# Token halves at the end of each output projection, and earlier evictions in the filter loop

## The reference, cut to what matters

```
x = x + (silu(h @ w_ffn_gate[l]) * (h @ w_ffn_up[l])) @ w_ffn_down[l]
return rmsnorm(x, norm_final)
...
a = attention(rms_norm(h, pre)) @ w_o
h = h + rms_norm(a, a_norm_post[l])
f = conv_ffn(rms_norm(h, ffn_norm_pre[l]))
h = h + rms_norm(f, ffn_norm_post[l])
...
def conv_ffn(x, w_in, conv_w, conv_b, w_out):
    u = x @ w_in
    u = causal depthwise conv of width 3 over tokens (u) + conv_b
    gate, val = jnp.split(u, 2, axis=-1)
    return (jax.nn.gelu(gate) * val) @ w_out
```

## Time and profile before

| what | value |
|---|---|
| median of 3 runs | 2651.42 us (2649.61 to 2651.51) |
| profiled execution, its own time | 2651.55 us |
| its span in the trace | 2649.7 us |
| PE busy | 2523.8 us, 95% of the span |
| POOL busy | 1615.3 us, 61% |
| DVE busy | 1382.1 us, 52% |
| ACT busy | 748.6 us, 28% |
| mean granted clock of PE | 0.982 of full speed |

### The profile page before, as it was taken

How to read it: one execution, slowest core, us unless ns; L and a number is a source line. 1 busy time by engine, 2 the same in 40 slices (tenths; PEclk the granted TensorE clock), 3 DMA queues, 4 the chain that set the end, 5 groups by cost and what they waited for, 6 DMA issues and landing times. The chain is left out here.

```text
span 2649.7 us, 37177 instructions
## 1 busy us (share of the span) xinstructions
PE 2523.8 (95%) x12786; PEld 2077.5 (78%) x12786; DVE 1382.1 (52%) x1995; ACT 748.6 (28%) x1398; POOL 1615.3 (61%) x1548
## 2 busy tenths in 40 slices
PE   8889999999999999999999799999999999999998
PEld 6678878788877888888777577888877777778886
DVE  6656675454423533320477658774064444687722
ACT  2255444001132221100334433331032222343300
POOL 6546555664544777777544267887763333778874
PEclk9999999999999999999999899999999999999999
DMA  4333323332222333323322122333222211233321
GB/s 140 120 96 100 95 84 95 89 92 68 68 64 98 93 95 98 96 96 99 108 64 65 36 78 82 99 95 99 85 76 81 68 64 48 84 87 95 98 96 64
DMA packets 235784, 229.20 MB, mean 86 GB/s; under 512 B 15809, under 2 KB 228289, under 8 KB 235665
## 3 DMA queue, kind: packets, MB, share of 16 engines
q1 hardware_dynamic: 212224, 204.72, 25.9%
q10 hardware_dynamic: 23440, 22.82, 3.0%
HBM read 222.67 MB, written 4.82 MB: 86 GB/s over the span
## 5 line engine op out<-in xcount | busy, mean ns | idle before, releaser
L583 POOL TENSOR_SCALAR whi<-raw 128x512 fp32r<-128x512 f32 x772 | 561.3, 727 | 943.9 <-issue 514.4
L585 POOL TENSOR_TENSOR wlo<-raw,whi 128x512 fp32r<-128x512 f32 x772 | 1055.7, 1368 | 64.4
L625 PE MATMUL PS<-opA_hi,whi 128*128 128x512 f32 x1872 | 751.5, 401 | 21.5 <-DVE fu L1939 9.5
L625 PE MATMUL PS<-opA_hi,wlo 128*128 128x512 f32 x1872 | 735.9, 393 | 0.0
L625 PE MATMUL PS<-opA_lo,whi 128*128 128x512 f32 x1872 | 735.5, 393 | 0.0
L625 PEld LDWEIGHTS PS<-opA_hi,whi 128*128 128x128 f32 x1872 | 356.0, 190 | 110.7 <-issue 21.6
L625 PEld LDWEIGHTS PS<-opA_hi,wlo 128*128 128x128 f32 x1872 | 355.1, 190 | 76.5
L625 PEld LDWEIGHTS PS<-opA_lo,whi 128*128 128x128 f32 x1872 | 356.0, 190 | 71.5 <-issue 1.5
L1949 DVE SCALAR_TENSOR_TENSOR facc<-fu,vec,facc 128x512 f32<-128x512 f32 x176 | 208.5, 1243 | 24.4 <-ACT facc L1322 24.2
L619 PE MATMUL PS<-whi,opA_hi 128*128 128x256 f32 x704 | 207.0, 294 | 0.0
L619 PE MATMUL PS<-whi,opA_lo 128*128 128x256 f32 x704 | 200.2, 284 | 0.0
(11 more groups left out here) (314 smaller groups left out, 3399.8 us busy)
## 6 DMA issues: line engine op xcount, KB each, us to landing
raw<-in_w_in_dram SPq DMA_DIRECT2D x184, 256.0 KB, 2.7
raw<-in_ffn_w_in_dram SPq DMA_DIRECT2D x176, 256.0 KB, 2.8
raw<-in_ffn_w_out_dram SPq DMA_DIRECT2D x88, 256.0 KB, 2.6
raw<-in_a_w_qkv_dram SPq DMA_DIRECT2D x48, 256.0 KB, 2.7
raw<-in_w_ffn_gate_dram SPq DMA_DIRECT2D x44, 256.0 KB, 2.8
raw<-in_w_ffn_up_dram SPq DMA_DIRECT2D x44, 256.0 KB, 2.8
raw<-in_w_ffn_down_dram SPq DMA_DIRECT2D x44, 256.0 KB, 2.6
acs_row<-acs_dram ACTq DMA_DIRECT2D x16, 512.0 KB, 5.9
```

Source lines behind the costliest of these rows:

```text
L583: nc.gpsimd.tensor_scalar(whi[slot][:], raw[raw_slot][:], 1.0, 1.0, ALU.mult, ALU.mult).then_inc(w_high, 1)
L585: nc.gpsimd.tensor_tensor(wlo[slot][:], raw[raw_slot][:], whi[slot][:].bitcast(F32), ALU.subtract).then_inc(slab_split, 1)
L625: last = nc.tensor.matmul(psum_fm(key, panel, m), a, b[:, k, :], start=k + n == 0, stop=k == total - 1 and n == 2)
```

## The change

The last tile (m = 1) of each of the five projections is computed in two halves of 256 tokens, the second into a bank of `AUX`; in the projections of eleven slabs this holds for all slabs of the last panel. The norm follows by halves: the factors of the first half are formed while PE computes the second, and DVE, ACT and PE treat the first two tiles (the first four at the end, k = 10) of the next operand in halves. `keep_warm` is gone from these boundaries. In the filter loop the eviction of half 1 moves from between the two `taps` of its own pass to the end of the pass before.

```diff
+HALVES = {2: 2, 4: 2, 6: 2, 8: 2, 10: 4}
+TOKENS = slice(0, HS), slice(HS, S)
...
+        def tail(key, h):
+            return psum_fm(key, 3, 1)[:, TOKENS[0]] if h == 0 else AUX[:, 0, TOKENS[1]]
...
+            def spread_late(k):
+                pe.wait_ge(rstd_ready, k + 1)
+                pe.wait_ge(half_res, HALF0[k] + HALVES[k])
+                for t in range(2, NB):
+                    last = nc.tensor.matmul(AUX[:, 3, t * P:(t + 1) * P], rstd_col[:, t:t + 1].broadcast_to([P, P]), ident[:], start=True, stop=True)
+                last.then_inc(bc_done, 1)
...
-            def branch_norm(k):
-                sum_squares(k)
-                keep_warm(WARM_FACTORS)
-                spread(k)
-                keep_warm(WARM_RESIDUAL)
...
+            def last_panel_norm(key, k):
...
+                for kk in range(first):
+                    s = slab_no(key, panel, kk)
+                    pe.wait_ge(slab_split, s + 1)
+                    for c in range(SLAB):
+                        products(psum_fm(key, panel, 0), s, c, 0, SLAB * kk + c, slice(0, S))
+                        for h in range(2):
+                            last = products(tail(key, h), s, c, 1, SLAB * kk + c, TOKENS[h])
...
             def prepare(k, dst, name, first, src_ready):
+                for c in range(HALVES[k - 1]):
+                    act.wait_ge(half_res, HALF0[k - 1] + c + 1)
+                    A(dst[:, c, TOKENS[0]], XT[:, c, TOKENS[0]], ACT.Copy, scale=col(name, first + c)).then_inc(half_hi, 1)
+                    if c == 0:
+                        norm_late(k - 1)
+                    A(next_squares[:, TOKENS[0], c], XT[:, c, TOKENS[0]], ACT.Square).then_inc(next_sq, 1)
...
+            def chunks(scale, add, k, ready0, nxt, first, late):
...
+                factors_half(k)
+                for c in range(H):
+                    scale(c, 0)
+                    if nxt and c:
+                        low_half(c - 1)
+                    add(c, 0)
+                    if c == 0:
+                        late()
+                factors_late(k)
                 if nxt:
+                    low_half(H - 1)
+                dve.wait_ge(bc_done, k + 1)
+                for c in range(DC):
+                    tokens = TOKENS[1] if c < H else slice(0, S)
+                    scale(c, 1 if c < H else None)
+                    if nxt and c:
+                        next_low(*nxt, c - 1, ready0, TOKENS[1] if c - 1 < H else slice(0, S))
+                    add(c, 1 if c < H else None)
...
+                def late():
+                    done(key, 3)
+                    dve.wait_ge(sq_ready, SQUARES0[k] + DC + 1)
+                    V.tensor_copy(branch[:, DC - 1, TOKENS[1]], tail(key, 1)).then_inc(tail_res, 1)
...
                 products(0)
+                evict(1, 1)
                 with dve.Fori(1, FP - 1) as i:
                     taps(i, 0)
-                    evict(i, 1)
                     taps(i, 1)
                     dve.wait_ge(fconv_tap, 88 * l + 8 * i + 4)
                     evict(i, 0, 1)
                     products(i)
+                    evict(i, 1, 1)
```

More of the change, by code:

```diff
@@ L624, in chunk @@
                     for n, (a, b) in enumerate(((ah, hi), (ah, lo), (al, hi))):
-                        last = nc.tensor.matmul(psum_fm(key, panel, m), a, b[:, k, :], start=k + n == 0, stop=k == total - 1 and n == 2)
+                        last = nc.tensor.matmul(psum_fm(key, panel, m)[:, tokens], a, b[:, k, tokens], start=tokens.start == 0 and k + n == 0,
+                                                stop=k == total - 1 and n == 2, skip_group_check=skip)
                 return last
@@ L634, in twin_mm @@
                 ready, base = FIRST_USE[key]
-                order = [(t, c) for c in range(total - 2) for t in (a, b)] + [(a, total - 2), (a, total - 1), (b, total - 2), (b, total - 1)]
+                first = 0
+                if norm in NEXT:
+                    first = HALVES[norm - 1]
+                    for h in range(2):
+                        for c in range(first):
+                            for t in (a, b):
+                                s = slab_no(*t, c // SLAB)
+                                if h == 0:
+                                    if c % SLAB == 0:
+                                        pe.wait_ge(slab_split, s + 1)
+                                    if t == a:
+                                        pe.wait_ge(half_op, HALF0[norm - 1] + c + 1)
+                                elif t == a:
+                                    pe.wait_ge(ready, base + c + 1)
+                                last = chunk(*t, s, c % SLAB, c, total, TOKENS[h], True)
+                                if h == 1 and c % SLAB == SLAB - 1:
+                                    last.then_inc(slab_done, 1)
+                            if h == 0 and c == 0:
+                                spread_late(norm - 1)
+                order = [(t, c) for c in range(first, total - 2) for t in (a, b)] + [(a, total - 2), (a, total - 1), (b, total - 2), (b, total - 1)]
                 for t, c in order:
@@ L709, in sum_squares @@
                 else:
-                    pe.wait_ge(acc_ready, ADDED0[k] + (DC - 1 if k in BRANCHES else DC))
+                    pe.wait_ge(acc_ready, ADDED0[k] + DC)
                 for t in range(NB):
-                    last = nc.tensor.matmul(AUX[:, 3, t:t + 1], acc[:, t * P:(t + 1) * P], ones[:, 0:1], start=t == 0, stop=k not in BRANCHES,
-                                            skip_group_check=True)
[L714 to L718, removed]
@@ L1872, in _, with next_low @@
             add_squares(2, 6)
-            done("down1", 3)
-            down_residual(7)
-            def next_low(name, first, c, ready0):
+            dve.wait_ge(tail_done, 1)
+            V.tensor_tensor(XT[:, DC - 1, TOKENS[0]], XT[:, DC - 1, TOKENS[0]], tail("down1", 0), ALU.add).then_inc(evicted, 1)
+            def next_low(name, first, c, ready0, tokens):
                 dve.wait_ge(res_ready, ready0 + c + 1)
-                low(opA_lo[:, c, :], XT[:, c, :], col(name, first + c), opA_hi[:, c, :])
@@ L1881, in chunks @@
[L1881 to L1890, removed]
-                if nxt:
-                    next_low(*nxt, DC - 1, ready0)
+                low(opA_lo[:, c, tokens], XT[:, c, tokens], col(name, first + c), opA_hi[:, c, tokens])
@@ L1901, in residual, with down_late @@
+            def down_late():
+                done("down1", 3)
+                V.tensor_tensor(XT[:, DC - 1, TOKENS[1]], XT[:, DC - 1, TOKENS[1]], tail("down1", 1), ALU.add).then_inc(tail_res, 1)
+            chunks(lambda c, h: None, final_norm, 2, 0, ("a_norm_pre_2", 0), (("q2", 0), [q2[0][:, m, :] for m in range(2)]), down_late)
             def residual(key, k, name, first, nxt, layer, first_panel):
```

173 lines of the change are left out of this document (136 added, 37 removed).

## The result

The changed kernel takes 2658.24 us (median of 9 runs, 2656.69 to 2659.53), the kernel before 2651.37 us (9 runs on the same chip, 2649.61 to 2653.74). The ratio is 1.0028, 95% interval 1.0018 to 1.0038, so it is about 7 us slower, which is clear of noise though small. The prediction was 2647.2. The profiled execution has a span of 2656.1 us, 6.4 more than before, and a mean granted clock of 0.977 where it was 0.982.

What follows compares the result with a forecast made beforehand. PE is busy 95% of the span, but DVE sets the end of the boundary stage. Terms -9.7 + 1.5 + 1.6 + 0.7 + 1.7 = -4.2 us give 2647.3, stated as 2647.2; own range 2644 to 2650, 8 in 10: 2641 to 2654.

Steps and rivals of the forecast that it cites:

- The step that failed: `bwo` boundary: PE ends 12 half products at 11.05, spreads the second half, DVE goes on at 11.75 after 0.6 idle.
- The second rival: Boundaries without constant matmuls: PE idles, the clock falls, each of four pays 1.7, +6.8 in all, 2654; chance 12%.
- the first scale: `bwo` boundary: DVE's first scale at 7.05 after tile m = 1 begins, 2.1 earlier than 9.18.
- the first product: `bwo` boundary: PE starts the next projection at about 9.6, 2.8 earlier than before.
- PE's head start: `bwo` boundary: PE's 2.8 us are given back whole to DVE; the stage ends 0.3 to 0.7 later.
- `awo`, `fout 0` and `bwo`: Boundaries behind these three projections: +0.5 each, +1.5 together, with POOL adding to DVE's extra half steps.
- Behind `down1`: Boundary after `down1`: +1.6, ACT on the path with an Exp and two table loads of 1.28.
- A last panel of eleven slabs: Split products of the first seven slabs, 42 in each of three projections: 0.55 longer each, +1.7 together.
- The end: End of the kernel (k = 10): +0.7, with 0.8 of DVE waiting for the late spread.
- the filter loops: Two filter loops with the moved eviction: gain of 4.85 each, -9.7, two waits of 1.2 to 2.4 replacing 4.75.
- no half-speed products behind: Sign in the filter loops: PE's remaining waits for the fu evictions are not followed by products at half speed.
- the attentions: Attentions 1 and 2: no term in the forecast sum; the result's table lists their forecast as 0.

Runs made afterwards that it cites:

- The kernel with the loop alone: Kernel before with only the new order of evictions in the filter loop, boundaries as before: 2641.95 us, ratio 0.9968.
- the two with the Exp moved: Changed kernel with constants in PE's waits, late spread sooner and two Exp ahead of `down1`'s squares: 2648.3 us; with both loop evictions early too: 2640.32 us.
- The token halves with the old loop: Changed kernel with the old order of evictions in the filter loop, so only the token halves remain: 2662.28 us, ratio 1.0039 to before.
- the kernel before with the prompt loop: Kernel before with both filter loop evictions as early as their panels are there, boundaries as before: 2640.1 us, ratio 0.9953.

## Why the prediction was wrong

**The step that failed** is in the boundary: "PE ends 12 half products at 11.05, then spreads the second half, so DVE can go on at 11.75: 0.6 idle". It takes PE at full clock behind the new waits. In the runs they are followed by half speed at all four boundaries of the changed kernel (behind `awo` from the fifth product on), and PE is on DVE's path here, through the late spread. So 12 products of 0.213 take 2.7 instead of 1.4 and the spread 0.3 more; DVE goes on at 13.44 and idles 2.37. With constants in the waits this is undone (11.89) and the whole kernel is level with before.

The second rival ("the clock falls in the new gaps", 12%, 2654) had the mechanism. It priced a boundary at 1.7, from the earlier trace rows; against my own steps the four measured 1.0 to 1.7 more each, 5.3 in all. The Trainium skill, page "TensorE: Matmul & The Clock Gate", section "What's actually happening", says that activity releases the throttle and that throttled is the default. By that rule the constants do work though they compute nothing; the run without them (+9.0) agrees. I had given the rule its 12% because I read the fall only behind the long gap. That was a misreading. The trace of before has it behind a wait of 2.45 us in attention 1 as well (granted clock 0.57 from 1507 to 1511; its PE rows are the last ones of this section). At the boundaries it could not show, because the constants stood there.

**Right:** the new places of the first scale (6.99 against 7.05) and of the first product (9.75 against 9.6), and that DVE gives PE's head start back. At full clock tile 7 ends 0.2 to 0.4 later than before behind `awo`, `fout 0` and `bwo`, where I took 0.5. Behind `down1` it is 1.6, as forecast, though its reason is only half right: 0.8 of it goes with the Exp. A last panel of eleven slabs takes 0.65 more, against 0.55. The end lost 1.2, against 0.7, and the clock is the reason there too. In the changed kernel the late spread takes 1.20, and DVE waits 1.31 for it where I took 0.8:

```profile
2643.39 1.20 PE L761 MATMUL AUX<-ident,rstd_col 128*128 128x128 f32 x4 [2.58 <-DVE rstd_col L1573]
2644.63 0.43 DVE L2074 TENSOR_TENSOR AUX<-branch,AUX 128x256 f32<-128x256 f32 x1 [1.31 <-PE AUX L761]
```

In three other kernels with this end the spread took 0.69 and DVE waited 0.80, and there the end lost 0.7.

**Mis-sized:** the filter loops, -9.7 forecast. The old waits of 4.75 went and waits of 2.13 came, inside the 1.2 to 2.4 given. In loop 1 that made -4.6. In loop 2 the clock fell behind the new wait, against "no half-speed products behind". PE and the windows of the changed kernel:

```profile
2341.34 0.47 PE L638 MATMUL PS<-opA_hi,whi 128*128 128x512 f32 x1 [2.13 <-DVE fu L2104]
...
2342.51 0.63 PE L638 MATMUL PS<-opA_lo,whi 128*128 128x512 f32 x1
2342.93 0.63 PE L638 MATMUL PS<-opA_hi,wlo 128*128 128x512 f32 x1
```

```profile
2338.00:2342.00 4.00, 1.87 (x9) 1.27 (x8) 4.00 (x5) 0.00 (x0) 3.58 (x3) 1.00 0.32 90
2342.00:2346.00 4.00, 4.00 (x13) 3.08 (x12) 3.39 (x6) 3.52 (x5) 0.00 (x0) 0.57 0.22 68
```

From the first of these products to tile m = 1 of the last panel PE takes 290.7 us, over the same stretch of loop 1 289.1: 1.6 of the 2.25 that are missing. The kernel with the loop alone has the same two waits and no fall, and gained 8.5.

**Not in the sum at all:** the attentions, +2.3 and +1.0. The changed kernel has a wait in attention 1 that is longer than its counterpart before, first the changed kernel, then before:

```profile
1510.20 0.71 PE L1092 MATMUL AUX<-v,pT 128*128 128x128 f32 x4 [2.46 <-ACT pT L1468]
...
1518.06 1.65 PE L1092 MATMUL AUX<-v,pT 128*128 128x128 f32 x6 [4.07 <-ACT pT L1468]
```

```profile
1507.43 1.22 PE L1003 MATMUL AUX<-v,pT 128*128 128x128 f32 x4 [2.45 <-ACT pT L1360]
...
1515.30 0.94 PE L1003 MATMUL AUX<-v,pT 128*128 128x128 f32 x6 [2.57 <-ACT pT L1360]
```

ACT and DVE keep the same distance in both. Before, PE ran at half clock behind the first wait (the four matmuls took 1.22) and filled the time; after, it ran at full clock (0.71), was done sooner, waited 4.07, and only then fell to half clock (1.65), where its products were on the path. Why the fall comes at the first wait in one kernel and at the second in the other is not shown by any run; that it is chance of timing is an argument only. The kernels with constants at the boundaries also waited 4.1 there. Their clock fell only 0.6 to 1.3 us behind the wait, where in the changed kernel it fell within it, and three of them lost only 0.7 to 0.8 in this stretch, the two with the Exp moved 1.45. The +1.0 of attention 2 goes with a second stretch below full clock (0.75, 0.67 and 0.90 from 1992 to 2004), but kernels with the old boundaries scatter by more there.

## What to carry to other kernels

Before matmuls on constants are taken out, ask what the products behind them do at half clock, and who waits for those: here taking them out cost 9.0 us (6.1 to 11.7). And a short step that another engine waits for should not be queued behind work that nobody waits for: the late spread six products sooner gave back some 3 us at the boundaries, where the constants gave 5.8. And where an eviction is late, put every eviction of the loop right where its panel is ready, not only the one that shows in the wait. The second was next in line: in the traces one edit shortened the loops by 4.7 and 4.2 us, both together by 7.1 and 6.7. A trace of one execution holds luck of the clock as well: stretches with the same code differed here by up to 1.9 us.

## What the runs showed of the hardware

The same short waits do not always bring the clock down. At each boundary of `awo`, `fout 0` and `bwo` without constants PE waits 0.47 and then 1.0 us, with two small sums of 0.6 between. Behind them products ran at half speed at all three in the changed kernel, and at two of three with the sooner spread. The token halves with the old loop stayed at full speed behind `fout 0` and `bwo`; this is `fout 0`:

```profile
1940.21 0.61 PE L752 MATMUL AUX<-ones,sq 128*128 128x1 f32 x4 [0.47 <-ACT sq L1421]
1941.83 0.35 PE L638 MATMUL PS<-opA_hi,whi 128*128 128x256 f32 x1 [1.01 <-DVE opA_lo L2003]
1942.02 0.28 PE L638 MATMUL PS<-opA_lo,whi 128*128 128x256 f32 x1
1942.13 0.28 PE L638 MATMUL PS<-opA_hi,wlo 128*128 128x256 f32 x1
```

A wait of 2.13 us (once 2.23) in the filter loop stands twice in each of six kernels. It was followed by half speed in five places of twelve, at 1.6 us each: in loop 2 of the changed kernel (0.57) and in both loops of the two kernels with constants, sooner spread and this loop order. Such a wait has no fixed price. Ahead of the first products of the next projection, waits of 2.45 to 3.3 us brought the fall every time (behind `down1` in the three token-half kernels without constants, and at all four boundaries of the kernel before without constants). The waits of 4.75 to 4.79 in the filter loop brought it six times of six. Elsewhere even such waits did not always do it: in attention 1 a wait of 2.45 us was followed by half speed before (1.22) and not in the changed kernel (0.71).

Nor do the constants hold the clock always. At the end of the kernel before with the prompt loop they are in place, and the spread still took 2.05 us instead of 1.16; the last add came 0.9 us later for it.
